# A transformer step with experts on one core: other first loads, and expert weights loaded during the output projection

## What is computed

```python
def trunk_layer(x, mod, ctx, ...):
    sh1, sc1, g1, sh2, sc2, g2 = jnp.split(mod, 6, axis=-1)       # mod = silu(c) @ w_ada + b_ada
    h = rmsnorm(x, n1) * (1.0 + sc1) + sh1
    mix, k_c, v_c, s_f, s_b = mixer(h, ctx, ...)    # h @ w_in; retention; differential attention;
    x = x + g1 * mix                                # gates; w_ret_o, w_diff_o, w_o
    h2 = rmsnorm(x, n2) * (1.0 + sc2) + sh2
    x = x + g2 * hier_moe(h2, ...)
    return x, k_c, v_c, s_f, s_b

def hier_moe(h, rgw, rgb, rew, reb, wg, wu, wd):
    # top-1 of 4 groups, top-2 of the 8 experts in it; 32 experts, FF = 256
    ...
    a = jax.nn.silu(jnp.einsum('nd,edf->nef', hf, wg)) * jnp.einsum('nd,edf->nef', hf, wu)
    y = jnp.einsum('nef,efd->nd', a * combine[:, :, None].astype(a.dtype), wd)
```

## Time and profile before

| | us |
|---|---|
| median of three runs | 1299.39 |
| lowest and highest | 1299.32, 1305.07 |
| the profiled execution | 1299.57 |
| its span | 1297.7 |

### The profile page before, as it was taken

The page is one execution under the profiler, slowest core; times in us unless marked ns, Lnnn a source line. Parts: engine busy times, 40 slices in busy tenths (PEclk is TensorE's granted clock), DMA queues, the critical chain, the costliest instruction groups (busy, mean ns, idle before and its releaser), DMA issues.

```text
span 1297.7 us, 19321 instructions
## 1 busy us (share of the span) xinstructions
PE 1124.4 (87%) x8087; PEld 912.6 (70%) x8087; DVE 496.1 (38%) x897; ACT 407.2 (31%) x870; POOL 94.4 (7%) x103
## 2 busy tenths in 40 slices
PE   2799999989998999999998999789995789777763
PEld 0488899989987898889997888689995333222221
DVE  0521114573343433442435555454547311111116
ACT  2522222211233544553226555421322121111113
POOL 0000001121000000000000111000002011111001
PEclk9799999999999999999999999999997899999997
DMA  8656632211311222232322111671217989999956
GB/s 302 232 169 205 227 100 66 66 50 57 98 56 60 58 78 78 62 94 86 94 74 70 49 54 49 238 277 65 98 49 284 383 349 419 421 421 421 421 235 240
DMA packets 90276, 222.32 MB, mean 171 GB/s; under 512 B 9881, under 2 KB 64962, under 8 KB 74706
## 3 DMA queue, kind: packets, MB, share of 16 engines
q1 hardware_dynamic: 85298, 209.60, 44.2%
q0 software_dynamic: 4608, 10.49, 2.1%
q10 hardware_dynamic: 288, 1.05, 0.2%
HBM read 206.40 MB, written 21.00 MB: 175 GB/s over the span
## 4 chain that ended last, share of the span: by engine, by line
PE 61%; DMA 13%; DVE 9%; issue 7%; ACT 6%; SPq 2%; POOL 1%; ACTq 0%; DVEq 0%; POOLq 0%
PE ps L883 41%; DMA arena<-in_moe_w_up 8%; PE ps L1113 6%; PE ps L1037 3%; PE ps L1126 2%; PE ps L1067 2%; DMA w_loaded<-in_w_in 2%; ACT arena L1394 2%; DVE w_low L1730 2%; PE ps L1051 2%; ACT w_high L1367 1%; PE ps L850 1%; DMA w_loaded<-in_w_diff_o 1%; DVE mx L1794 1%; DVE mx L1795 1%
## 5 line engine op out<-in xcount | busy, mean ns | idle before, releaser
L883 PE MATMUL ps<-w_high,h_high 128*128 128x256 f32 x1280 | 370.3, 289 | 9.9 <-DVE arena L1627 5.2
L883 PE MATMUL ps<-w_low,h_high 128*128 128x256 f32 x1280 | 363.6, 284 | 0.0
L883 PE MATMUL ps<-w_high,h_low 128*128 128x256 f32 x1280 | 363.5, 284 | 0.0
L883 PEld LDWEIGHTS ps<-w_high,h_high 128*128 128x128 f32 x1280 | 247.1, 193 | 24.4 <-ACT arena L1334 10.1
L883 PEld LDWEIGHTS ps<-w_low,h_high 128*128 128x128 f32 x1280 | 247.2, 193 | 0.2
L883 PEld LDWEIGHTS ps<-w_high,h_low 128*128 128x128 f32 x1280 | 246.9, 193 | 0.0
L1730 DVE TENSOR_TENSOR w_low<-w_loaded,w_high 128x2048 fp32r<-128x2048 f32 x44 | 100.8, 2291 | 173.9 <-ACT w_high L1367 173.8
L1113 PE MATMUL ps<-arena 128*64 128x512 f32 x512 | 121.1, 628 | 24.1 <-DMA arena<-in_moe_w_up 16.9
L1334 ACT COPY arena<-ps 128x256 f32<-128x256 f32 x100 | 37.3, 373 | 249.2 <-PE ps L883 249.2
L1113 PEld LDWEIGHTS ps<-arena 128*64 128x64 f32 x512 | 39.9, 145 | 103.2 <-issue 103.2
L1367 ACT CAST w_high<-w_loaded 128x2048 fp32r<-128x2048 f32 x44 | 83.8, 1905 | 64.5 <-DMA w_loaded<-in_w_o 40.0
(11 more groups left out here) (268 smaller groups left out, 1702.0 us busy)
## 6 DMA issues: line engine op xcount, KB each, us to landing
w_loaded<-in_w_in SPq DMA_DIRECT2D x32, 1024.0 KB, 5.7
arena<-in_moe_w_gate SPq DMA_DIRECT2D x32, 1024.0 KB, 14.3
arena<-in_moe_w_up SPq DMA_DIRECT2D x32, 1024.0 KB, 20.4
arena<-in_moe_w_down SPq DMA_DIRECT2D x32, 1024.0 KB, 21.3
arena<-in_w_ada SPq DMA_DIRECT2D x24, 1024.0 KB, 5.6
gates<-arena SPq DMA_DIRECT2D x40, 128.0 KB, 1.7
arena<-y_rows SPq DMA_DIRECT2D x10, 512.0 KB, 8.2
arena<-in_x_sample SPq DMA_DIRECT2D x8, 512.0 KB, 10.9
```

The source lines that it names most:

```text
L883: mm = pe.matmul(out[:, 0:N256], x[:, t, k * P:(k + 1) * P], w[i % 2][:, k, :], start=(k == 0 and j == 0), stop=(k == KC - 1 and j == 2))
```

## The change

The head's loads come in another order, with semaphores of their own for the rows, the biases and one table of constants. The biases are broadcast to two partitions of each 32 instead of all, over a memset. DVE's low part of the first unit comes before `ada_rows_out(0)`. The ring for POOL's DMA descriptors shrinks from 16 to 4 KB per partition, and the arena grows to 210 KB; tiles of the router's stage move into the new 12 KB and into the place of constants, which frees 118 to 138 and 158 to 162 KB before the router. Expert 5 is loaded after the transposes of `wo0` and the gate and up parts of expert 2 at the end of the first half of `wo1`. The router's preparation moves from `wd0` to `wd1`.

```diff
-        arena = sb("arena", [P, 198 * KB])
+        arena = sb("arena", [P, 210 * KB])
...
-        x1T = [at(118 + 4 * i, D).rearrange("p (k t) -> p k t", k=KC) for i in range(2)]
-        x1_square = at(126, D)
+        x1T = [at(198 + 4 * i, D).rearrange("p (k t) -> p k t", k=KC) for i in range(2)]
...
-        h2 = [at(158, D), at(80, D)]
+        h2 = [at(206, D), at(80, D)]
...
-        w_dn = [at(k, 2 * D).rearrange("p (k n) -> p k n", k=2) for k in (44, 68, 102, 110, 20, 154)]
+        w_dn = [at(k, 2 * D).rearrange("p (k n) -> p k n", k=2) for k in (44, 68, 102, 110, 20)]
+
+        w_dn.append(arena[:, 134 * KB:(134 + 48) * KB].rearrange("p (k n) -> p k n", k=2)[:, :, 0:D])
...
+        x1_square = masks[:, 1000:1000 + D // 2].bitcast(BF16)
...
-            if item[0] == "mm" and item[1:] in (("wd0", 1, 1), ("wd0", 2, 1), ("wd0", 3, 1), ("wd0", 4, 1)):
+            if item[0] == "mm" and item[1:] in (("wd1", 1, 0), ("wd1", 2, 0), ("wd1", 3, 0), ("wd1", 4, 0)):
                 plan.append(("W", item[2] - 1))
...
+            sp.wait_ge(pool_set, 1)
             for j in range(4):
                 src = a["b_ada"][0].rearrange("(r j n) -> j r n", r=3, j=4)[j]
-                sp.dma_start(bias_rows[32 * j:32 * j + 32, :, :], src.partition_broadcast(32)).then_inc(ld_small, 16)
...
+                sp.dma_start(bias_rows[32 * j:32 * j + 2, :, :], src.partition_broadcast(2)).then_inc(ld_bias, 16)
+            for i in range(2, KC - 2):
                 load_ada(i)
             load_w(0)
+            for i in range(KC - 2, KC):
+                load_ada(i)
             load_w(1)
...
                     elif n == last_of["wo1"]:
                         sp.wait_ge(pe_dense, n + 1)
-                        load_expert(2, 2)
+                        load_down(2, 2)
                         load_expert(3, 3)
+                    elif item == ("mm", "wo1", PT, 0):
+                        sp.wait_ge(pe_dense, n + 1)
+                        load_gate_up(2, 2)
                     elif item == ("T4", "m", PT, 1):
...
+                        load_expert(5, 5)
 
             sp.wait_ge(pe_logits, NT)
-            load_gate_up(5, 5)
             load_down(4, 4)
             sp.wait_ge(h2_ready, NT)
             load_gate_up(4, 4)
-            sp.wait_ge(st_h2[0], 16 * 3)
-            load_down(5, 5)
...
-            act.wait_ge(ld_small, 16 * 16)
+            act.wait_ge(ld_rows, 16 * 6)
...
+            low_weights(0)
             ada_rows_out(0)
...
+            pool.memset(bias_rows, 0.0).then_inc(pool_set, 1)
...
-    nc = bacc.Bacc("TRN2", target_bir_lowering=False, num_devices=1)
+    nc = bacc.Bacc("TRN2", target_bir_lowering=False, num_devices=1, dynamic_dma_scratch_size=4096)
```

More of the change, by code:

```diff
@@ L445, in build @@
             emit(item)
-            if item[0] == "mm" and item[1:] in (("wd0", 1, 1), ("wd0", 2, 1), ("wd0", 3, 1), ("wd0", 4, 1)):
+            if item[0] == "mm" and item[1:] in (("wd1", 1, 0), ("wd1", 2, 0), ("wd1", 3, 0), ("wd1", 4, 0)):
                 plan.append(("W", item[2] - 1))
-            if item == ("mm", "wd1", 2, 0):
+            if item == ("mm", "wd1", 3, 1):
                 plan.append(("LB",))
@@ L526, in build @@
         ld_const, ld_small, ld_x = sem("ld_const"), sem("ld_small"), sem("ld_x")
+        ld_rows, ld_bias, ld_setup = sem("ld_rows"), sem("ld_bias"), sem("ld_setup")
         ld_w = [sem("ld_w0"), sem("ld_w1")]
@@ L586, in _ @@
                           (32, a["ret_norm_g"][0])):
[L587 to L590, removed]
+                sp.dma_start(rows[r0:r0 + 8, :], vec(v)).then_inc(ld_rows, 16)
+            sp.dma_start(rows[40:41, :], vec(a["diff_subln_g"][0])).then_inc(ld_rows, 16)
+            sp.dma_start(const[:], a["const"][:, setup_n:]).then_inc(ld_const, 16)
+            for t in range(NT):
+                src = a["x_prompt"][0] if t == PT else a["x_sample"][0][t * P:(t + 1) * P, :]
+                sp.dma_start(xn[:, t, :], src).then_inc(ld_x, 16)
             def load_ada(i):
@@ L605, in _ @@
                 load_ada(i)
+            sp.dma_start(const0, a["const"][:, 0:setup_n]).then_inc(ld_setup, 16)
+            sp.dma_start(dec[:, 0:4], a["ret_decay_fwd"][0].partition_broadcast(P)).then_inc(ld_small, 16)
+            sp.dma_start(dec[:, 4:8], a["ret_decay_bwd"][0].partition_broadcast(P)).then_inc(ld_small, 16)
             for i, v in enumerate(("diff_lambda_q1", "diff_lambda_k1", "diff_lambda_q2", "diff_lambda_k2")):
                 sp.dma_start(lam_in[:, i, :], a[v][0].partition_broadcast(P)).then_inc(ld_small, 16)
+            sp.wait_ge(pool_set, 1)
             for j in range(4):
                 src = a["b_ada"][0].rearrange("(r j n) -> j r n", r=3, j=4)[j]
-                sp.dma_start(bias_rows[32 * j:32 * j + 32, :, :], src.partition_broadcast(32)).then_inc(ld_small, 16)
[L611 to L614, removed]
+                sp.dma_start(bias_rows[32 * j:32 * j + 2, :, :], src.partition_broadcast(2)).then_inc(ld_bias, 16)
+            for i in range(2, KC - 2):
                 load_ada(i)
             load_w(0)
+            for i in range(KC - 2, KC):
+                load_ada(i)
             load_w(1)
@@ L836, in _ @@
             ident = C("ident")
-            pe.wait_ge(ld_const, 32)
+            pe.wait_ge(ld_const, 16)
             pe.wait_ge(dve_set, 1)
@@ L1250, in _ @@
             act.wait_ge(dve_set, 5)
-            act.wait_ge(ld_const, 32)
+            act.wait_ge(ld_setup, 16)
             for h in range(8):
@@ L1567, in ada_rows_out, with low_weights @@
                 dve.tensor_copy(dst, src).then_inc(mod_cols, 1)
+            def low_weights(i):
+                dve.wait_ge(w_rounded, i + 1)
+                dve.tensor_tensor(w_lo[i % 2][:], w_raw[i % 2], w_hi[i % 2][:].bitcast(F32), ALU.subtract).then_inc(w_split, 1)
+            low_weights(0)
             ada_rows_out(0)
@@ L1727, in _ @@
                 elif e[0] == "cv":
-                    i = e[1]
-                    dve.wait_ge(w_rounded, i + 1)
-                    dve.tensor_tensor(w_lo[i % 2][:], w_raw[i % 2], w_hi[i % 2][:].bitcast(F32), ALU.subtract).then_inc(w_split, 1)
+                    if e[1]:
+                        low_weights(e[1])
                 elif e[0] == "ada":
```

14 lines of the change are left out of this document (7 added, 7 removed).

## The result

The changed kernel takes 1305.22 us (median of 20 runs, 1299.91 to 1309.7), the kernel before 1300.12 us beside it on the same chip (20 runs, 1296.61 to 1306.59). The ratio is 1.0034, 95% interval 1.0023 to 1.0045: slower by 4.4 us, 3.0 to 5.8, which is clear of noise and within the 0.5% that the prediction counts as no change. The profiled execution took 1302.87 us (span 1301.0), 3.3 us more than the one of before.

What follows compares the result with a forecast made beforehand. Dense projections bound by PE up to 984 us, then experts, whose weight loads PE's events issue. Head -2.1, `w_o` stall with clock +5.1, gather -2.1 gave +0.9 on 1299.57: 1300.5 us, range 1289.5 to 1305.5.

Steps and rivals of the forecast that it cites:

- 5.1 - 2.1: Expert edits: 5.1 us lost to the stall before the second half of `wo0` and its clock, 2.1 gained at the gather.
- The 12.4 us of loads are worth 0: Expert stage: taking five loads (5.24 MB, 12.4 us) out of the queue at 984 us gains 0 directly.
- Gather, -2.1: Before pair 0: the gather of token rows lands sooner behind a shorter queue, gain 2.1 us (0 to 5.5).
- The `w_o` load, landing at 942.5: Near 944 us: expert 5's loads ahead delay this load to 942.5, stalling PE 2.8 us (2.1 to 3.4).
- The clock behind that stall, +2.3: After the pause near 944 us: PE at 1.2 instead of 2.4 GHz, costing 2.3 us, lower end 1.3.
- The head, -2.1: Kernel start: reordered loads, smaller biases and earlier weight preparation gain 2.1 us (from -3.4 to +1.0).
- +2.5 for `w_in` ahead of two slices: Head: the first `w_in` load ahead of the last two `w_ada` slices delays the last slice by 2.5 us.
- -0.4 for ScalarE's and VectorE's order: Head: casting and subtracting the first weights before the wait for `w_ada` gains some 0.4 us.
- -4.2 us that stood against it: Head: constant tables +1.4, smaller biases -2.9, large loads beginning earlier -1.1, DMA dip covered by token rows -1.6.
- A: Rival, expert stage: DMA bounds it all, so the tail gains the full 12.4 us; 1290.2 us, chance 0.15.
- B: Rival: `w_o` load not held up, or moving loads does nothing; only head and gather gains left; 1295.4 us, chance 0.14.
- C: Rival, near 944 us: expert 5's load itself is slow, 13.1 us, adding 5.5 us of stall; 1306.0 us, chance 0.08.

Runs made afterwards that it cites:

- e_experts: The changed kernel with the head of before: early expert loads, router's preparation, places and smaller ring remain; 1302.38 us, 1.0012 of the kernel before.
- e_late5: As e_experts, but expert 5's three loads are issued behind the `w_o` load, not ahead of it; 1299.09 us, 0.9991 of the kernel before.
- e_head: The kernel before with the change's head edits alone (load order, small biases, `low_weights(0)` early); 1303.31 us, 1.0025 of the kernel before.
- e_head_lowlate: As e_head, but first `w_in` load behind all eight `w_ada` slices and `low_weights(0)` back behind the `w_ada` product; 1299.23 us, 0.9981 of the kernel before.
- e_best1: The kernel before with early expert loads as in e_late5 and all six expert weight slots in rotation; 1295.57 us, 0.9969 of the kernel before.
- e_best2: e_head_split's head on the kernel before, expert 5 behind the `w_o` load, expert 4 behind the first gather, six slots rotating; 1288.83 us, ratio 0.9905.
- e_head_split: As e_head_lowlate, with row loads and ten small broadcasts on ScalarE's queue, two `w_ada` slices ahead of token rows; 1293.45 us, 0.9943 of the kernel before.
- e_head_act: As e_head, but `w_in` behind all `w_ada` slices and ten small broadcasts on ScalarE's queue; 1302.63 us, 1.0020 of the kernel before.

## Why the prediction was right, and where it wasn't

The verdict (no change that counts) and the range held, the size didn't: +0.9 was forecast and +4.4 measured. That the range held is luck in part, for its upper end lies 0.3 us above the median and below the 1306.3 that the prediction's own terms reach. The head was 5.3 us dearer than its term, the experts' edits some 1.4 us cheaper than theirs (+1.6 us, 0 to 3.3, in `e_experts`, for 5.1 - 2.1), and one cost was put at nothing, the half clock in pair 0's product.

- **The 12.4 us of loads are worth 0.** Right, and the central step: the queue ran dry at 1013, and the time from pair 0's to the last product didn't fall (231.2 us for 229.2). `e_late5` shows it without the stall.
- **Gather, -2.1.** Right: -1.8 in the profile, 7.12 us for 6.8. Its reason was right too: 8.91 with the full queue, 7 with the shorter, 4.15 with an empty one. What the term left out is that pair 0's product then runs longer at half clock, 9.99 us for 8.49 here, and it is the end of this product that issues the next load: 1.5 of the 1.8 us were lost again in this pair of profiles.
- **The `w_o` load, landing at 942.5.** Right: issued 931.49, landed 944.77, less the 2.1 us that all was late, 942.7. The stall of +2.8 came as +3.0. The Trainium skill ("DMA: Bandwidth & Descriptors", "Where 436 GB/s comes from") would have it at 943.6 with its 358 GB/s; the trace stands with its own 421.
- **The clock behind that stall, +2.3.** Not in the profile of the change, behind 3.0 us of pause; there in that of `e_experts`, behind 3.7 us (11.27 for 8.89 us, +2.4). The lower end should have been 0 and not 1.3. Half clock came elsewhere, but not all of it is the change's: the first dense product took 0.7 us longer (5.20 for 4.51, where the six kernels with the head of before take 4.46 to 5.46), pair 0's 1.5, and the product at 835 us 1.6, which the wait for `w_diff_o` took in (its landing at 870.3 was 2.4 us late, the stage before it 2.1).
- **The head, -2.1.** This step failed: +3.2 us (2.0 to 4.7) in `e_head`, and +1.8 in the profile of the change. Its +2.5 for `w_in` ahead of two slices was right as far as two profiles tell (38.73 to 41.41, +2.7; 42.46 in `e_head`), and the -0.4 for ScalarE's and VectorE's order has its sign (from the last product to the first dense one 11.09 us, 10.14 in `e_head`, for 11.27). What failed is the -4.2 us that stood against it (1.4 - 2.9 - 1.1 - 1.6). `e_head_lowlate` has exactly those, and gains 1.4. Two things took the rest. The dip isn't covered by the token rows: I took it for a queue without large transfers, and it is the small transfers themselves. It came with 3 MB issued behind it just as well, 70 to 155 GB/s in 18 to 20.5 us, and cost some 1.9 us against 421 GB/s, where a gain of 1.6 was put down. And the saved time didn't all reach `w_ada`. The packets of the trace tell the loads apart, 8 KB for `w_ada` and 1 KB for `w_in`: up to 30 us `e_head_lowlate` has moved 5.86 MB of `w_ada` and the kernel before 4.61, which is 3.0 us at 421 GB/s, but 0.94 MB of `w_in` had gone by when its last `w_ada` product started, where before it was 0.36, which is 1.4 us. The first piece of `w_in` moved 3.9 us ahead of that product and not 1.2, though its load stands behind all the slices in the queue. The sum took the queue's loads as finished one after the other.

What in these ten loads holds up the DMA was not taken apart. The share of busy DMA engines in the dip is 0.25 to 0.32 (18 to 20 us), and the biases, cut to two partitions each, are the loads that changed. The Trainium skill ("DMA: Bandwidth & Descriptors", "Why a DMA increments its semaphore by 16 and not by 1") says that a transfer goes over the largest number of engines, up to 16, that divides the slowest dimension on both sides, which would be two for a load of two partitions. The low share fits that, but no run here isolates one such load, and the dip of before, with biases of 32 partitions, had shares down to 0.05.

Of the rivals, A fell in the change, `e_experts`, `e_late5` and `e_best1`; B's point (the load isn't held up) is what `e_late5` makes true by an edit; C's cause didn't occur, for the DMA moved 389 GB/s from 935 to 943 us, while expert 5 was landing, though the time it named, 1306.0, is close to what came, for other reasons.

## What to carry to other kernels

Loading earlier pays only where a wait ends on that load; in a stage whose loads are issued by consumed buffers, look for the moments in which no buffer is free, and give the queue work there (4.6 us by rotation, against 0 by 12.4 us of loads moved). A latency-bound transfer that everybody waits for, such as a gather, should find the queue empty: hold back bulk loads that aren't due (2.8 us here). Edits of one diff can depend on each other; price each without the others, and ask of a DMA dip whether the queue lacks work or is working on something small. And take several executions of the same code before a difference of 1 or 2 us between two profiles is given a cause.

## What was not expected of the hardware

- The clock fell behind pauses of PE of 4.4 us and 3.7 us (`e_experts`), behind one of 3.1 us at 872 us in the change, and not behind those of 3.0 us at 946 us in the change and at 872 us in `e_late5`. How much it costs varies: behind the same pause of 3.5 us near 828 us the next product takes 3.11 us before and 4.70 in the change. Beside that, executions of the same code differ: the head of `e_late5` is the kernel before's, yet from its first dense product to the second it takes 7.35 us (52.20 to 59.55) and not 6.41 (51.35 to 57.76), at half clock for longer. Such episodes are worth 0.7 to 2.4 us each, so a difference of 2 us at one place between two profiles is no more than a hint.
- Moving the small loads of the head to ScalarE's queue, with two slices of `w_ada` first, took 7.3 us off the median. Up to the first dense product one profile shows 1.6 us of that and the other, of `e_best2`, 4.3.
- A load can take time from the one ahead of it in its queue: 0.94 MB of `w_in` moved before the last slice of `w_ada` was used in `e_head_lowlate`, 1.94 MB in `e_head_split`, 0.36 MB before.
- The granted clock reads 1.00 where the record has no entry yet (`e_head_split`, 0 to 54 us); the spacing of the matmuls, 0.21 or 0.12 us here, tells which level it was.
- Four loads of 12 KB to two partitions each took SyncE 3.84 us to issue, while those of 192 KB had taken 1.90 us. On ScalarE's queue the same four took 1.7 us (`e_head_act`) and 1.4 (`e_head_split`), so it isn't the loads alone.
